# Nine item widths in place of five in the expert part of a two-layer encoder

## The reference

```python
def moe_swiglu(h, w_router, w_gate_e, w_up_e, w_down_e):
    b, s, d = h.shape
    xt = h.reshape(-1, d)
    logits = (xt @ w_router).astype(jnp.float32)
    top_val, top_idx = lax.top_k(logits, TOP_K)          # TOP_K = 2, N_EXPERTS = 8
    gates = jax.nn.softmax(top_val, axis=-1)
    flat_e = top_idx.reshape(-1)
    order = jnp.argsort(flat_e)
    tok = order // TOP_K
    sizes = jnp.bincount(flat_e, length=N_EXPERTS).astype(jnp.int32)
    xs = xt[tok]
    hg = lax.ragged_dot(xs, w_gate_e, sizes)             # 1024 -> 3584
    hu = lax.ragged_dot(xs, w_up_e, sizes)
    ys = lax.ragged_dot(jax.nn.silu(hg) * hu, w_down_e, sizes)   # 3584 -> 1024
    ys = ys * gates.reshape(-1)[order][:, None].astype(ys.dtype)
    out = jnp.zeros_like(xt).at[tok].add(ys)
    return out.reshape(b, s, d)
```

## Time and profile before

| | us |
|---|---|
| median of 3 executions | 3488.38 (3488.0 to 3492.32) |
| the profiled execution | 3493.34 |
| its span | 3491.8 |
| TensorE busy (share of the span) | 3442.3 (99%) |
| VectorE busy | 2043.4 (59%) |
| ScalarE busy | 1563.0 (45%) |
| items begin on TensorE at | 1491.6 |

### The profile page before, as it was taken

How to read it: one execution, slowest core, us unless ns; L and a number is a source line. 1 busy time by engine, 2 the same in 40 slices (tenths; PEclk the granted TensorE clock), 3 DMA queues, 4 the chain that set the end, 5 groups by cost and what they waited for, 6 DMA issues and landing times.

```text
span 3491.8 us, 68944 instructions
## 1 busy us (share of the span) xinstructions
PE 3442.3 (99%) x25495; PEld 3243.7 (93%) x25495; DVE 2043.4 (59%) x3129; ACT 1563.0 (45%) x2335; POOL 221.4 (6%) x259
## 2 busy tenths in 40 slices
PE   9999899999999999999999999999999999999998
PEld 8888799999999899799999999999999898898886
DVE  6455577766544556454455455446555587686774
ACT  4455433333333433354344344445454465554653
POOL 1000000000100000022010001001010020010100
PEclk9999899999999999999999999999999999999999
DMA  5111332222553423266455445456566575665654
GB/s 199 38 51 41 137 117 73 85 83 84 200 186 117 137 67 110 105 201 182 152 183 193 163 164 200 164 168 228 192 223 207 187 244 195 202 231 190 228 198 155
DMA packets 159181, 548.23 MB, mean 157 GB/s; under 512 B 23345, under 2 KB 23353, under 8 KB 159056
## 3 DMA queue, kind: packets, MB, share of 16 engines
q1 hardware_dynamic: 123248, 444.67, 38.8%
q0 software_dynamic: 32352, 95.54, 7.8%
q10 hardware_dynamic: 3456, 6.29, 0.5%
HBM read 508.20 MB, written 59.08 MB: 162 GB/s over the span
## 4 chain that ended last, share of the span: by engine, by line
PE 96%; DVE 2%; ACT 1%; issue 1%; DMA 0%; DVEq 0%; SPq 0%; POOL 0%; POOLq 0%; ACTq 0%
PE ps L342 77%; PE ps L2494 8%; PE ps L2495 4%; PE ps L738 1%; PE ps L809 1%; PE ps L821 1%; PE ps L2418 1%; PE ps L839 0%; PE ps L829 0%; ACT eA L878 0%; DMA yT<-in_xT 0%; PE ps L762 0%; PE ps L1207 0%; PE ps L1994 0%; PE ps L2448 0%
## 5 line engine op out<-in xcount | busy, mean ns | idle before, releaser
L328 DVE TENSOR_TENSOR wl<-wraw,wh 128x1024 fp32r<-128x1024 f32 x800 | 979.3, 1225 | 887.1 <-ACT wh L324 878.0
L324 ACT ACTIVATE wh<-wraw 128x1024 fp32r<-128x1024 f32 x796 | 841.0, 1057 | 930.0 <-PE ps L342 867.1
L342 PE MATMUL ps<-ex,wh 128*128 128x256 f32 (+2 forms) x4484 | 850.7, 289 | 1.1 <-DVE wl L328 1.1
L342 PEld LDWEIGHTS ps<-ex,wh 128*128 128x128 f32 x4484 | 704.4, 188 | 1.5 <-issue 1.4
L342 PE MATMUL ps<-ex,wl 128*128 128x288 f32 (+2 forms) x2240 | 647.1, 289 | 0.0
L2494 PE MATMUL ps<-ex,wh 128*128 128x480 f32 x1344 | 445.2, 382 | 0.0
L342 PEld LDWEIGHTS ps<-ex,wl 128*128 128x128 f32 x2240 | 420.6, 188 | 0.0
L342 PE MATMUL ps<-xs,wh 128*128 128x256 f32 x2432 | 388.9, 282 | 4.3 <-DVE qAl L865 1.9
L342 PE MATMUL ps<-bc,wh 128*128 128x256 f32 (+1 forms) x2496 | 386.6, 277 | 0.0
L2495 PE MATMUL ps<-ex,wl 128*128 128x240 f32 x1344 | 366.5, 273 | 0.0
L342 PEld LDWEIGHTS ps<-xs,wh 128*128 128x128 f32 x2432 | 327.0, 190 | 15.9 <-issue 9.9
(11 more groups left out here) (390 smaller groups left out, 4773.9 us busy)
## 6 DMA issues: line engine op xcount, KB each, us to landing
wraw<-in_w_expert SPq DMA_DIRECT2D x676, 512.0 KB, 3.3
wraw<-in_w_main SPq DMA_DIRECT2D x164, 512.0 KB, 3.8
act_d<-ast POOLq DMA_DIRECT2D x22, 512.0 KB, 2.9
araw<-act_d POOLq DMA_DIRECT2D x22, 512.0 KB, 5.1
hT<-h_d POOLq DMA_DIRECT2D x4, 2048.0 KB, 14.3
h_d<-hT POOLq DMA_DIRECT2D x3, 2048.0 KB, 9.6
hT<-in_xT POOLq DMA_DIRECT2D x2, 2048.0 KB, 9.6
xrow_d<-rows ACTq DMA_DIRECT2D x16, 256.0 KB, 2.1
```

Of the source, the lines that this page charges most:

```text
L324: act.activation(wh[:, j], wraw[:, j], ACT.Copy).then_inc(hi_done, 1)
L328: dve.tensor_tensor(wl[:, j], wraw[:, j], wh[:, j].bitcast(F32), ALU.subtract).then_inc(lo_done, 1)
L342: mm = pe.matmul(out[:, s], a, b[:, s], start=first and part == 0 and c == 0, stop=last and part == 2 and d == n)
```

## The change

The table of widths gets four more entries, so each of the three engines holds nine copies of the item code in place of five. A padding tile shrinks by the four words that `upto` grows.

```diff
-WIDTHS = (CAP, 304, 288, 256, 240)
+WIDTHS = (CAP, 320, 304, 296, 288, 280, 272, 256, 240)
...
         upto = sb("upto", [1, len(WIDTHS) + 1], I32)
-        sb("spare", [1, 39], I32)
+        sb("spare", [1, 35], I32)
```

## The result

The changed kernel takes 3549.68 us (median of 5 runs, 3544.47 to 3554.91), the one before 3488.38 (3486.91 to 3493.9). The ratio is 1.017, its 95% interval 1.0156 to 1.0184. The forecast was 3491, its range ended at 3501.

A forecast was written before the change was run, and what follows sets the result against it. TensorE, busy 99% of the span, was taken as the bound, with stands at branches. Terms -13.5 + 12.8 + 3.2 = +2.5 us gave 3490.9 beside the median 3488.38, taken as 3491; range 3479 to 3501.

The forecast's parts named there:

- What it removes: Gain from narrower items: first from 304 to 296 columns, third from 288 to 280, others unchanged; 13.5 us in sum.
- The first item's 5.7 us: Saving of the first item, 304 to 296 columns, from the slope between the measured widths 304 and 288.
- widths off the grid save nothing: Rival: 296 and 280, no multiples of 16, cost like 304 and 288; +16.0 us, 3504.4; chance 0.10.
- The third item's 7.8 us: Saving of the third item, 288 to 280 columns, taken between bounds of 5.7 and 10.0 us.
- 280 goes with 256: Rival: 280 columns pace like 256, so the third item saves 19.8 us; -9.5 us, 3478.9; chance 0.10.
- Loads ahead of the first item, 3.0 us: Before the first item: 2.6 us for TensorE's four added loads, 0.4 for VectorE's compares and sum.
- VectorE decides, 9.8 us: Before the first item, TensorE waits while VectorE passes empty copies 320 and 304; 9.8 us, bounds 8.0 and 14.7.
- no term of its own: TensorE's own branches over 320 and 304 add nothing while they stay below VectorE's delay.
- the start's 12.8 us: Total added ahead of the first item: 3.0 for loads and compares plus 9.8 for VectorE; bounds 11.0 and 17.7.
- The branch over 272, 3.2 us bare: Between third and fourth items, TensorE's branch takes 4.0 us, 3.2 of it bare (1.8 to 3.5); VectorE's is hidden.
- The clock, taken as 0: Half clock after TensorE's second stand before its fifth unit: no loss taken, 2.5 us only in the upper bound.
- The rival taken from the Trainium skill: Branches are cheap: a target inside fetched blocks needs no wait on the engines; -7.7 us, 3480.7; chance 0.10.

The follow-up runs named there:

- e2: The kernel before with only its spare tile grown from 39 to 47 words, tiles behind it 32 bytes later; 3546.0 us, ratio 1.0163.
- e1: The changed kernel with its spare tile cut from 35 to 31 words, putting the products' tiles back at their old addresses; 3502.85 us, ratio 1.004 to the kernel before.
- e6: The kernel before with widths 384, 296, 288, 280, 256, 240, no empty copy but that of 384, tiles in place; 3482.77 us, ratio 0.9979.
- e5: The kernel before with one more width, 280, which is used, and no empty copy but that of 384; 3480.53 us, ratio 0.9975.
- e4: The kernel before with two more empty copies, 320 and 272, no item's width changed and tiles in place; 3501.08 us, ratio 1.004.

## Why the prediction was wrong

**The step that failed** is a term put at nothing without a reason. "What it removes" let all items but two, and everything ahead of them, keep their time ("the others keep their width"). The second line of the diff was taken for neutral, a tile that shrinks by the words that another grows. It moved nearly all tiles by 32 bytes against the weights. e2 puts this at +56 us, e1 takes 46.8 of it back. Most of the 9 us between the two comes from the first item's width. The shift makes 296 columns faster, 136.9 ns when shifted and 139.8 in place (1096 and 1073 matmuls in 150 us, shown at the end), and 304 slower, 138.4 in place and 139.8 shifted; over 2016 matmuls these are 5.9 and 2.8 us.

The remaining terms can be read from e1, where the forecast of +2.5 meets +12.9 (medians). By e6, the two widths gain some 7 us in place of 13.5, and the empty copies cost 20 in place of 16.

*The first item's 5.7 us.* Wrong in sign. By the slope between 288 and 304 a matmul of 296 columns would be 2.8 ns shorter than one of 304. It is 1.3 to 1.4 longer (in 150 us 1073 in e1 and 1074 in e6, against 1084), so 2016 of them cost some 2.7 us more than at 304. The rival "widths off the grid save nothing" held for 296, but not for 280. The prediction noted that eight columns were no measured width; its range should have carried a loss there.

*The third item's 7.8 us.* Right, 9.0 measured in e5, inside the 5.7 to 10.0. The rival "280 goes with 256" fell: it wanted 19.8.

*Loads ahead of the first item, 3.0 us.* Right: ten loads take from 1475.9 to the branch at 1482.6, 6.7 us for what took 4.1 before.

*VectorE decides, 9.8 us.* Mis-sized, and the wrong engine. Its two added copies took 5.6 us. Their branches took 1.9 and 1.1, below the lower bound of 2.6. The DMA share beside them did fall, as forecast. But the share does not order TensorE's branches, 4.26 us at 0.70 and 4.18 at 0.16. Windows of e1 over TensorE's first two branches, then over VectorE's second and third (PE, PEld, DVE, ACT, POOL, clock, DMA share, GB/s):

```profile
1482.63:1486.88 4.25, 0.00 (x0) 0.00 (x0) 1.65 (x9) 1.49 (x2) 1.91 (x2) 0.50 0.70 253
1489.25:1493.43 4.18, 2.01 (x15) 1.77 (x13) 4.02 (x8) 4.12 (x8) 3.47 (x3) 0.91 0.16 53
...
1502.65:1504.58 1.93, 1.51 (x7) 1.39 (x7) 0.00 (x0) 0.00 (x0) 0.00 (x0) 0.50 0.02 6
1505.86:1506.95 1.09, 1.09 (x6) 1.09 (x5) 0.00 (x0) 0.00 (x0) 0.00 (x0) 0.50 0.00 0
```

So why a branch takes as long as it does is not shown. What delayed the items was TensorE itself, whose added branches took 4.18 and 6.66 us and which the prediction called "no term of its own". That the start's 12.8 us came near the 11.2 measured is luck: it was worked out through VectorE. So is the first matmul at 1500.8, where the prediction had put it (1501), since longer branches met an execution that was 2.0 us ahead. The fifth unit never waited for VectorE; the wait for L328 that e1 has, 3.3 us, ends at 2340.83 us, where VectorE's low part was done at 2339.9 and TensorE's own branch over 272 ended at 2340.2.

*The branch over 272, 3.2 us bare.* Right in place and size: 3.5 (e4), 3.3 (e1). VectorE's is hidden there, as forecast.

*The clock, taken as 0.* Mis-sized. A stand of 3.5 us was enough for 6.8 us at the 1.2 GHz level, which costs 2.8 at the fourth item, and the stand ahead of the first item is followed by half clock to 1507.0, 6.2 us into the item. With the 2.7 us of the width, and less the wait of 1.1 for VectorE that is gone, this is what makes the first item 4.0 longer.

The rival taken from the Trainium skill (Runtime: NRT & Kernel Launch, "Instruction fetch mechanics"), that a branch to a target inside the fetched blocks is cheap, did not come about on TensorE: all of its branches over about 1,150 instructions, less than the 2048 that the page says it holds, took 3.4 to 6.7 us in the changed kernel and in e1. No row shows how many of those instructions lie ahead of a branch. On VectorE the later branches over 150 instructions were partly cheap: 2.2 us between its tests at 2339.1 and 2341.3 in e1, the loads included. But the same place took 5.6 us in e4 (2334.6 to 2340.2). Which blocks VectorE holds at a branch was not tried.

Still open: why the distance between the two groups of tiles sets the pace, which pair of tiles it is, and whether it has a period. Distances beyond 128 bytes were not tried.

## What to carry to other kernels

Before a change is judged by what it does, compare where the tiles lie: a few words more in one small tile cost 1.6% here, and a window of code that the change doesn't touch shows it at once. The cause is shown by e1 and e2 together: the shift alone brings the loss, and taking it back removes most of it. A width that is meant to save columns must be timed at its own placement, since pace is not a straight line in the columns. A copy of code that is never entered costs TensorE its branch and then the clock, so only widths in use pay. Which are in use depends on the counts, which the program can't know: the 9 us of e5 hold for these inputs.

## What the runs showed of the hardware

The pace of these fp32 matmuls depends on the distance in bytes between the weights' tiles and the tiles that are multiplied with them. At 256 columns it is 113.5 ns at the kernel's own distance, 118.4 at 32 bytes more, 120.0 at 64, 117.8 at 96 and at 128, and 118.9 at 64 bytes less (2643, 2534, 2500, 2547, 2546 and 2523 matmuls in 300 us). Moving both groups together by 64 bytes changes nothing (2643). Neither 64 nor 128 bytes is a period of it.

What a distance is worth depends on the width. At 288 columns 32 bytes more make no difference and 64 bytes more are better (1128 and 1142 matmuls in 150 us, 1127 at the old distance). At 512 columns 32 bytes more are worse (148 against 150 in 34 us). At 296 columns 32 bytes more are better (1096 matmuls in 150 us in the changed kernel, 1073 in e1). None of the distances tried is the best for all widths.

```profile
1560.00:1710.00 150.00, 150.00 (x1096) 1.00 0.60 181
```

```profile
1530.00:1680.00 150.00, 150.00 (x1073) 1.00 0.57 173
```
